# Expert weights handed over in the order of use: one 2 MB load holds the same half of both experts of a pair

## The reference

```python
for i in range(DEPTH):                       # DEPTH = 2
    x = x + mixer_i(rmsnorm(x, norm_mix[i]))
    x = x + moe_ffn(rmsnorm(x, norm_ffn[i]), router_w, router_b,
                    moe_w_gate[i], moe_w_up[i], moe_w_down[i])
# in moe_ffn: gates are zero except for a token's two experts
hg = jnp.einsum('td,edf->tef', xt, w_gate)   # 16 x 2048 x 512
hu = jnp.einsum('td,edf->tef', xt, w_up)     # 16 x 2048 x 512
a = jax.nn.silu(hg) * hu * gates[..., None]
y = jnp.einsum('tef,efd->td', a, w_down)     # 16 x 512 x 2048
```

## Time and profile before

| | |
|---|---|
| three runs | 1660.14, 1661.31, 1664.47 us (median 1661.31) |
| the profiled execution | 1661.03 us, its span 1659.3 us |
| TensorE (PE) busy | 1611.1 us, 97% |
| VectorE, ScalarE busy | 758.6 us (46%), 482.1 us (29%) |
| DMA | 535.84 MB, mean 323 GB/s |
| 2 MB loads of expert weights, issue to landing | medians of 21.4 to 33.0 us |

### The profile page before, as it was taken

One profiled execution on the slowest core, in us unless ns is written; L12 is line 12 of the kernel. 1 busy time (PEld: TensorE's weight loads), 2 busy tenths in 40 slices (PEclk: granted clock), 3 DMA queues, 4 the chain that ended last, 5 costly groups with the idle time before them and its releaser, 6 DMA issues.

```text
span 1659.3 us, 19405 instructions
## 1 busy us (share of the span) xinstructions
PE 1611.1 (97%) x8014; PEld 1010.1 (61%) x8014; DVE 758.6 (46%) x1316; ACT 482.1 (29%) x622; POOL 44.9 (3%) x26
## 2 busy tenths in 40 slices
PE   9999999999999999889999999999999999989898
PEld 8888888887433434333459999888754344333343
DVE  5885477744332222212267777684532322222223
ACT  6444456434000000000054565564320000000000
POOL 0000000000000000000040000020000000000000
PEclk9999999999999999999999999999999999999999
DMA  9755656577999999999995545554799999999998
GB/s 368 268 189 166 198 166 197 171 264 298 421 415 425 428 427 427 428 429 425 420 360 174 152 137 158 190 179 151 290 423 421 423 427 428 428 427 428 427 422 342
DMA packets 110441, 535.84 MB, mean 323 GB/s; under 512 B 8704, under 2 KB 28048, under 8 KB 77840
## 3 DMA queue, kind: packets, MB, share of 16 engines
q1 hardware_dynamic: 109920, 534.04, 82.0%
q10 hardware_dynamic: 432, 0.53, 0.1%
HBM read 532.43 MB, written 2.11 MB: 322 GB/s over the span
## 4 chain that ended last, share of the span: by engine, by line
PE 81%; DMA 15%; DVE 2%; ACT 1%; SPq 1%; issue 1%; DVEq 0%; ACTq 0%
PE PS L806 33%; PE PS L1173 21%; PE PS L1218 8%; DMA DOUBLE<-in_moe_w_down 5%; DMA DOUBLE<-in_moe_w_up 5%; PE PS L927 2%; PE PS L1079 2%; DMA SPARE<-in_moe_w_gate 2%; PE PS L1237 2%; DMA OVD<-in_moe_w_gate 2%; PE PS L1116 2%; PE PS L1117 1%; PE PS L933 1%; DMA ring<-in_a_w_in 1%; PE PS L1099 1%; PE PS L1004 1%
## 5 line engine op out<-in xcount | busy, mean ns | idle before, releaser
L1173 PE MATMUL PS<-DOUBLE,AREA 128*64 128x512 f32 x1264 | 336.1, 597 | 10.8 <-DMA OVD<-in_moe_w_gate 5.4
L1834 DVE TENSOR_TENSOR LO<-ring,HI 128x2048 fp32r<-128x2048 f32 (+1 forms) x122 | 262.4, 2151 | 168.1 <-ACT HI L1459 167.6
L806 PE MATMUL PS<-HI,XT_BOTH 128*128 128x512 f32 (+1 forms) x1344 | 298.0, 373 | 1.1 <-issue 0.6
L1459 ACT ACTIVATE HI<-ring 128x2048 fp32r<-128x2048 f32 (+1 forms) x122 | 219.8, 1802 | 272.4 <-PE PS L806 234.5
L806 PEld LDWEIGHTS PS<-HI,XT_BOTH 128*128 128x128 f32 x1344 | 244.1, 188 | 35.5 <-issue 2.4
L1173 PEld LDWEIGHTS PS<-DOUBLE,AREA 128*64 128x64 f32 x1264 | 107.6, 139 | 196.0 <-issue 195.7
L1173 PE MATMUL PS<-OVD,AREA 128*64 128x512 f32 x400 | 179.2, 599 | 0.0
L806 PE MATMUL PS<-LO,XT_BOTH 128*128 128x512 f32 (+1 forms) x672 | 152.5, 368 | 0.0
L2243 DVE TENSOR_TENSOR AREA<-PS,SMALL 128x512 f32<-128x512 f32 x64 | 44.1, 689 | 236.3 <-PE PS L1079 203.0
L1218 PE MATMUL PS<-DOUBLE,AREA 128*64 128x512 f32 x528 | 143.4, 599 | 3.6 <-DMA DOUBLE<-in_moe_w_down 3.2
L1645 ACT ACTIVATE AREA<-PS 128x512 f32<-128x512 f32 x16 | 9.6, 597 | 438.7 <-PE PS L1173 438.7
(11 more groups left out here) (325 smaller groups left out, 1847.3 us busy)
## 6 DMA issues: line engine op xcount, KB each, us to landing
DOUBLE<-in_moe_w_up SPq DMA_DIRECT2D x26, 2048.0 KB, 24.3
DOUBLE<-in_moe_w_gate SPq DMA_DIRECT2D x24, 2048.0 KB, 21.4
DOUBLE<-in_moe_w_down SPq DMA_DIRECT2D x24, 2048.0 KB, 28.5
ring<-in_a_w_in SPq DMA_DIRECT2D x47, 1024.0 KB, 5.2
DOUBLE<-in_moe_w_gate SPq DMA_DIRECT2D x30, 1024.0 KB, 13.3
DOUBLE<-in_moe_w_up SPq DMA_DIRECT2D x24, 1024.0 KB, 15.1
ring<-in_b_w_in SPq DMA_DIRECT2D x32, 768.0 KB, 4.4
OVD<-in_moe_w_up SPq DMA_DIRECT2D x9, 2048.0 KB, 29.1
```

The lines of the kernel that those rows point to most:

```text
L806: mm = pe.matmul(PS[:, banks[t], 0:n], lhs(k0 + kk, t)[part], weights[:, kk, 0:n], start=first and kk == 0 and p == 0, stop=last and kk == ...
L1173: last = pe.matmul(PS[64 * e:64 * e + 64, up, :], tokens_of(c, e), slot(units[e])[:, kk, :], start=(c == 0), stop=(c == DC - 1))
L1459: act.activation(HI[s % 2][:, :, 0:n], ring[PLACE[u]][:, :, 0:n], ACT.Copy).then_inc(sem("hi_ready"), 1)
L1834: tt(LO[PLACE[u]][:, :, 0:n], ring[PLACE[u]][:, :, 0:n], HI[s % 2][:, :, 0:n], ALU.subtract)\
```

## The change

All expert weights are laid out on the host in one tensor, `in_experts`, by layer, pair and block of 4 MB, in rows of 32 KB for a partition: half 0 of expert 0, half 0 of expert 1, half 1 of expert 0, half 1 of expert 1. A 2 MB load takes 16 KB of each row, which is the same half of both experts, so units are used in the order of their numbers and `in_turn` goes. Before, a 2 MB load read one contiguous block. Singles are now only units 22 to 33 (and the same early ones as before) and the last 8 down units; the last pair's 16 gate and up units come in doubles, the last in two pieces of 1 MB. TensorE's groups and matmuls, the slots and the early loads are the same.

```diff
-FINE = 56
+FINE = 34
 SINGLES = ({6, 7, 10, 11, *range(WIDE + ONCE, FINE)}, {6, 7, 10, 11, 12, 13, 14, 15, *range(WIDE + ONCE, FINE)})
-LAST_UPS = (13, 15)
+LAST_UPS = (14, 15)
-def in_turn(k):
-    return k if k >= BY_COLUMNS else k // 4 * 4 + (0, 2, 1, 3)[k % 4]
...
-    return expert(u) and (k in singles or k >= PAIRS * PAIR_UNITS - HALVES)
+    return expert(u) and (k in singles or k >= BY_COLUMNS)
...
-        def half(v, k):
+        def half(v, k, n=1):
-            return v[:, UNIT_K * UNIT_C * k:UNIT_K * UNIT_C * (k + 1)]
+            return v[:, UNIT_K * UNIT_C * k:UNIT_K * UNIT_C * (k + n)]
-        def expert_sources(wg, wu, wd, i):
...
+        def two_units(layer, i, n):
+            return half(w["experts"][layer, i, n // 2], 2 * (n % 2), 2)
...
                 def room(k, units):
-                    last = max(in_turn(before_in_slot(k + n)) for n in range(units))
+                    last = max(before_in_slot(k + n) for n in range(units))
                     sp.wait_ge(used, base + last + 1)
...
-                for k in sorted(range(EARLY, FINE), key=lambda k: in_turn(before_in_slot(k))):
+                for k in sorted(range(EARLY, FINE), key=before_in_slot):
                     room(k, 1)
                     single(base + k, all_of[k // 2])
...
-                for k in sorted(range(PAIRS * PAIR_UNITS - HALVES, PAIRS * PAIR_UNITS), key=in_turn):
+                for k in range(PAIRS * PAIR_UNITS - HALVES, BY_COLUMNS, 2):
+                    room(k, 2)
+                    if k - front != LAST_UPS[0]:
+                        double(base + k, all_of[k // 2])
+                    else:
+                        src = all_of[k // 2].rearrange("p (e k) -> p e k", e=2)
+                        for h in range(2):
...
-                                units = [8 * q + 4 * up + 2 * e + k for e in range(2)]
+                                units = [8 * q + 4 * up + 2 * k + e for e in range(2)]
...
-                        units = [16 + 4 * (c // 2) + 2 * e + c % 2 for e in range(2)]
+                        units = [16 + 2 * c + e for e in range(2)]
...
+def expert_rows(inputs):
+    gate, up, down = (np.asarray(inputs[n]) for n in ("moe_w_gate", "moe_w_up", "moe_w_down"))
+    rows = np.empty((2, PAIRS, PAIR_UNITS // 4, P, 2, 2, UNIT_K * UNIT_C), np.float32)
+    for i in range(PAIRS):
+        n, h = divmod(i, 2)
+        for e in range(2):
+            x = PER_GRP * (2 * h + e) + n
+            for q in range(2):
+                for at, a in ((2 * q, gate), (2 * q + 1, up), (4 + q, down)):
+                    rows[:, i, at, :, :, e] = a[:, x].reshape(2, 2, P, 2, -1)[:, q]
+    return rows.reshape(2, PAIRS, PAIR_UNITS // 4, P, 4 * UNIT_K * UNIT_C)
```

More of the change, by code:

```diff
@@ L591, in single @@
                         .then_inc(sem(f"unit_loaded_{PLACE[u]}"), 16)
-                first = list(expert_sources(wg, wu, wd, 0))
+                first = [two_units(layer, 0, n) for n in range(PAIR_UNITS // 2)]
                 def early(k):
@@ L622, in experts @@
                 early_half(11)
-                single(base + WIDE + ONCE, list(expert_sources(wg, wu, wd, 0))[(WIDE + ONCE) // 2])
+                early_half(WIDE + ONCE)
                 if layer == 0:
@@ L631, in experts @@
                 early(WIDE + 2)
-                all_of = [src for i in range(PAIRS) for src in expert_sources(wg, wu, wd, i)]
-                for k in sorted(range(EARLY, FINE), key=lambda k: in_turn(before_in_slot(k))):
+                all_of = [two_units(layer, i, n) for i in range(PAIRS) for n in range(PAIR_UNITS // 2)]
+                for k in sorted(range(EARLY, FINE), key=before_in_slot):
                     room(k, 1)
@@ L644, in experts @@
                 front = PAIRS * PAIR_UNITS - PAIR_UNITS
-                for k in sorted(range(PAIRS * PAIR_UNITS - HALVES, PAIRS * PAIR_UNITS), key=in_turn):
-                    room(k, 1)
[L647 to L655, removed]
-                                src = half(all_of[(front + n) // 2], n % 2)
-                                rows = slice(2 * h, 2 * h + 2)
-                                sp.dma_start(in_double(base + front + n)[:, rows, :].rearrange("p k c -> p (k c)"),
-                                             src[:, 2 * h * UNIT_C:2 * (h + 1) * UNIT_C])\
-                                    .then_inc(sem(f"unit_loaded_{PLACE[base + front + n]}" if h else "last_ups_begun"), 16)
+                for k in range(PAIRS * PAIR_UNITS - HALVES, BY_COLUMNS, 2):
[5 more added lines that the diff above has]
+                        for h in range(2):
+                            rows = slice(2 * h, 2 * h + 2)
+                            sp.dma_start(DOUBLE[PLACE[base + k]][:, :, rows, :].rearrange("p e k c -> p e (k c)"),
+                                         src[:, :, 2 * h * UNIT_C:2 * (h + 1) * UNIT_C])\
+                                .then_inc(sem(f"unit_loaded_{PLACE[base + k]}" if h else "last_ups_begun"), 16)
+                for k in range(BY_COLUMNS, PAIRS * PAIR_UNITS):
+                    room(k, 1)
+                    d, c = divmod(k - BY_COLUMNS, 2)
+                    sp.dma_start(in_double(base + k).rearrange("p k c -> p (k c)"), w["last_down"][layer, d, c])\
+                        .then_inc(sem(f"unit_loaded_{PLACE[base + k]}"), 16)
             a_in = k_view(w["a_w_in"][0])
@@ L700, in _ @@
                 unit(U_CKV + n, b_in[n][:, :, Q_COLS:Q_COLS + RANK])
-            sp.wait_ge(used, U_MOE0 + max(in_turn(last_in(RING + n)) for n in range(2)) + 1)
+            sp.wait_ge(used, U_MOE0 + max(last_in(RING + n) for n in range(2)) + 1)
             sp.dma_start(b_["WKR"], w["b_w_in"][0].rearrange("(c p) n -> p c n", p=P)[:, :, Q_COLS + RANK:])\
@@ L759, in _ @@
                                 j = q * PAIRS + 2 * i + h
-                                whole = list(expert_sources(wg, wu, wd, (i, h)))
-                                srcs = [half(whole[2 * b + e], k) for b in range(PAIR_UNITS // 4) for k in range(2) for e in range(2)]
+                                srcs = [half(two_units(l, 2 * i + h, n // 2), n % 2) for n in range(PAIR_UNITS)]
                                 for n, src in enumerate(srcs):
@@ L1138, in opening @@
                             last = pe.matmul(PS[64 * e:64 * e + 64, 0, :], tokens_of(c, e),
-                                             slot(2 * e)[:, c, :], start=(c == 0), stop=False)
+                                             slot(e)[:, c, :], start=(c == 0), stop=False)
                             if c == UNIT_K - 1:
@@ L1263, in overflow @@
                             gather_some(m, g)
-                            pair(m, j, g, 0, lambda n: pe.wait_ge(sem(f"over_loaded_{l}_{order(n) % 4}"),
-                                                                  16 * (PAIR_UNITS // 4) * k + 16 * (order(n) // 4 + 1)),
-                                 lambda n: OV[order(n) % 4], sem(f"over_free_{l}"), False, False)
+                            pair(m, j, g, 0, lambda n: pe.wait_ge(sem(f"over_loaded_{l}_{n % 4}"),
+                                                                  16 * (PAIR_UNITS // 4) * k + 16 * (n // 4 + 1)),
+                                 lambda n: OV[n % 4], sem(f"over_free_{l}"), False, False)
                     gather(m, gather_turn(l, MIDDLE), (0, 1))
```

35 lines of the change are left out of this document (8 added, 27 removed).

## The result

Timed side by side, the changed kernel takes 1669.58 us at the median (1667.45 to 1671.4, 5 runs) and the kernel before 1662.23 us (1660.14 to 1664.47, 5 runs): a ratio of 1.0043, 95% interval 1.003 to 1.0056. The forecast of +5.3 us is a ratio of 1.0032, inside both intervals, and both times are inside its range. Each execution has its own mean granted clock, and in the first timing the time goes with it: 1667.45 and 1668.47 us at 0.999, 1669.58 and 1670.03 us at 0.997, 1671.4 us at 0.995. In the second all eight stood at 0.998 or 0.999 (1667.26 to 1669.47 us), so about 1668 us is the time of the change at full clock.

What follows compares the result with a forecast made beforehand. The DMA stream of expert loads was taken to bound both layers. Layer 0: +4.4 - 1.4 - 0.5 - 0.2 = +2.3 us; layer 1: +4.4 - 1.4 = +3.0; together 1666.6 us, 8-in-10 range 1657.5 to 1670 us.

Steps and rivals of the forecast that it cites:

- The bound: Both layers: the end moves with the time the unbroken stream of expert loads gets to the last pair.
- When the loads may start: Near 470 and 1274 us: the double for units 40 and 41 waits, the DMA queue runs dry; +4.4 us a layer.
- I see one gap a layer: Loads queued behind the late double are issued in time, so DMA has only one gap in each layer.
- Fewer, larger loads: Units 34 to 55 and the last pair: 18 joins of 1 MB loads at 0.07 us; -1.4 us a layer.
- Order of arrival: Groups need one double instead of two, but the lead ends where the last pair begins; 0 us.
- rival C: The lead of one load gets to the end: 1651 us, or 1659 us with the gap; chance 0.07.
- Layout: Expert loads read 16 KB rows 32 KB apart; the spacing costs little or nothing, taken as 0.
- D: Rival: the new rows are slower to read, under 424 GB/s from 560 to 640 us; +15.9 us, 1677 us; chance 0.09.
- Near gap, spare time: Layer 0: the near gap at the double issued at 510.5 us goes, -0.5 us; 0.2 us to spare at layer's end.
- The sum: Layer 0 +2.3 us and layer 1 +3.0 us, together +5.3 us: 1666.6 us; chance 0.55.
- B: Rival: no gap in DMA's stream, only the joins count; -3.3 us, 1658 us; chance 0.15.
- E: Rival: the gap in one layer only, or some 2 us each; about 1662 to 1664.5 us; chance 0.14.

Runs made afterwards that it cites:

- run 7: Also e7_gap_doubled: the changed kernel, but the 2 MB load for units 40 and 41 waits one group longer in each layer; 1673.63 us, ratio 1.0066.
- run 1: The changed kernel with 1 MB loads for units 22 to 51 and not only to 33 (FINE = 52); 1660.21 us, ratio 0.9987.
- e2_old_layout_fine34: Also run 2: the kernel before with FINE = 34, so old layout and order with 2 MB loads from unit 34 on; 1669.58 us, ratio 1.0048.
- e8_change_again: The changed kernel unedited, timed and profiled a second time; 1668.14 us, ratio 1.0033.
- run 3: The changed kernel with units 40, 41, 50 and 51 as single 1 MB loads in both layers; 1665.79 us, ratio 1.0028.
- run 9: The changed kernel with units 34 to 41, 50 and 51 as 1 MB loads, 42 to 49 in four 2 MB loads; 1666.11 us, ratio 1.0022.
- run 10: The changed kernel with units 34 to 39 in three 2 MB loads, 40 to 51 in twelve 1 MB loads; 1660.06 us, ratio 0.9988.
- Run 6: The changed kernel with FINE = 52 and the last pair's gate and up units in 1 MB loads again; 1661.45 us, ratio 0.9998.
- e11_fine52_again: Run 11: the changed kernel with 1 MB loads for units up to 51 (FINE = 52), measured again; 1660.07 us, ratio 0.9987.

## Why the prediction was right, point by point

*The bound* (the end stands on the unbroken stream of loads, in both layers): right. It is what the account above says, and run 7 moved the end by 5.5 us when one wait of SP's queue was lengthened in each layer, 6.6 us of idle time.

*When the loads may start*, +4.4 us a layer: right in cause and place, and a little small. The double was issued at 470.38 us (forecast 470.35), the windows lose 4.9 us of DMA time, and taking the doubles away (run 1) gives 8 us back. Two numbers inside the term were off, with opposite signs. The landing behind the gap took 7.3 us, not the 8.4 read from the earlier trace rows: 2.4 us over its bytes, under even the lower bound of 2.7. (In `e2_old_layout_fine34` and `e7_gap_doubled` the same load took 8.0 and 7.9 us.) The Trainium skill's page DMA: Bandwidth & Descriptors (section "Anatomy of one DMA") has 2.0 us there, fitted for another issue path; 7.3 us is nearer to it than to my rows, though an estimate by its number alone would have put the gap at 2.9 us. Against that, the load behind the double was put at nothing and came 1.3 us late, so the third double landed at 489.06 us in `e8_change_again` (489.05 us in the change) where an unbroken stream (469.4 + 3 x 4.9) has 484.1: 5.0 us late, not 4.4. That the two nearly cancel is luck.

One more thing I had not read: the 16 engines don't run dry together. In `e8_change_again` the share falls through 0.77, 0.39 and 0.15 in half-microsecond windows from 465.5 us on and is 0 from 468.5 us, while the load itself lands at 469.5. So the landing of one load does not say how long the mean engine stands idle.

*"I see one gap a layer"*: nearly right for the change in layer 0 (423 GB/s from 475 us on in `e8_change_again`, 1.3 us more by one landing), less so in layer 1 (2.2 us more). The reason given, that the loads behind are issued in time, was too simple. With the gap itself closed, the four doubles of units 42 to 49 still cost some 3 us a layer ((1665.79 - 1660.21) / 2 in run 3, (1666.11 - 1660.07) / 2 in run 9). A change repaired at the gap alone I would have put some 3 us too low, as the expectation of run 3 was (2.8 us over its range).

*Fewer, larger loads*, -1.4 us a layer: in the last pair the size of a join is about right (0.09 us against 0.07 to 0.08), as far as two sessions can say. For units 34 to 51 it was wrong: the three joins of run 10 saved nothing that shows, and those of units 42 to 49 cost some 3 us a layer.

*Order of arrival*, 0: right. In the last pair TensorE still waits for loads, and the chain goes through them until 1633.87 us; rival C is out. Run 6 agrees (0.9998 of the kernel before).

*Layout*, 0: right, by 428 GB/s from 560 to 640 us (D wanted under 424) and by run 2. The Trainium skill's page DMA: Bandwidth & Descriptors (section "Latency and other measured facts") warns of slow HBM rows at large powers of two, from 512 KiB on; at 32 KB no run here shows any slowing.

*Near gap, spare time*, -0.5 and -0.2 us: not measured by themselves.

*The sum*: +5.3 us was forecast; the two timings give +7.1 and +5.5 us (ratio less 1, times 1661.31), both inside the +3.3 to +8 of the mechanism. That the second is so near is partly luck, as the gap cost more than its term and the joins of units 34 to 51 gave nothing. Rivals B (no gap) and E (part of a gap) are out by the windows. What the first timing has above the second goes with the mean granted clock of its runs, as said above; only one of the five has a trace, and there it is the fall near 1220 us, worth about 4.0 us. In the others the place of the fall is not known.

## What to carry to other kernels

Where DMA is the bound and its queue is short, load size is a matter of when slots come free, not of efficiency: one 2 MB load instead of two of 1 MB saved about 0.09 us where the queue was long, while nine such loads a layer cost about 4 us where the queue was short: one waited 3.4 us for its second slot, and four came late in a short queue. Look for the place where SP's issues come only as fast as slots are freed, keep loads small just there, and put one more load ahead of it if a slot can be found. Judge a gap by the DMA share of narrow windows, not by the landing of one load, and look at the rate beside the share too.

## What the runs showed of the hardware that I had not expected

- **A full share is not a full rate.** In runs 3 and 9 four 2 MB loads issued one by one into a short queue moved 370 to 398 GB/s at a share of 0.97 to 1.02; in run 10 the same bytes at the same place moved 419 to 424 GB/s in 1 MB loads. Why is open: with a gap ahead of them (`e8_change_again`) the same doubles kept 419 to 423 GB/s.
- **TensorE's clock fell to 1.2 GHz in a busy stretch**, for about 10 us near 1220 us, in the profiles of the change and of run 9 (mean granted clock 0.85 and 0.83 from 1200 to 1230 us); in the other profiles it was at full speed there. TensorE's busy time doesn't tell the two apart: `e8_change_again` was busy 2.98 of the 4 us from 1218 us and kept its clock, the change 3.53 of them. What sets it off was not tried.
- **The time of a run goes with its mean granted clock.** Runs 10 and 11 were at 0.999 in all 22 executions and spread over 1659.66 to 1661.38 us; the kernel before beside them was at 0.993 to 0.998 and spread over 1659.92 to 1666.2 us in 29. In run 6 the nine executions at 0.998 or 0.999 took 1660.77 to 1662.13 us, the three at 0.996 or 0.997 took 1664.07 to 1666.3 us. In the trace of the kernel before the clock is 0.97 from 650 to 800 us, where TensorE waits for loads up to 2.7 us at a time; in `e11_fine52_again`, whose waits are 1.3 us at most, it is 1.00 there, with TensorE as busy (136.0 and 135.9 us of these 150). Whether the shorter waits keep the clock up was not tried.
